# The start of a two-block transformer kernel: two product units formed from gained but unscaled x, with x loaded in chunks and the weight queue started at once

## The reference

```
def _rmsnorm(x, g, eps=EPS):
    xf = x.astype(jnp.float32)
    y = xf * lax.rsqrt(jnp.mean(xf * xf, axis=-1, keepdims=True) + eps)
    return (y * g.astype(jnp.float32)).astype(x.dtype)
...
        h = _rmsnorm(x, g_mix_pre[l])
        proj = h @ w_in[l]
...
    wl, al, gl = xs[..., o2:o3], xs[..., o3:o4], xs[..., o4:]
```

## Time and profile before

| what | us |
|---|---|
| median of 3 runs | 3977.71 (3976.71 to 3978.68) |
| the profiled execution | 3979.2 |
| its span | 3977.4 |
| TensorE busy | 3846.1 (97%) |
| VectorE, POOL, ScalarE busy | 1747.7, 1233.2, 599.5 |
| DMA moved | 668.80 MB, mean 168 GB/s |

### The profile page before, as it was taken

How to read it: one execution, slowest core, us unless ns; L and a number is a source line. 1 busy time by engine, 2 the same in 40 slices (tenths; PEclk the granted TensorE clock), 3 DMA queues, 4 the chain that set the end, 5 groups by cost and what they waited for, 6 DMA issues and landing times.

```text
span 3977.4 us, 65016 instructions
## 1 busy us (share of the span) xinstructions
PE 3846.1 (97%) x28196; PEld 3553.6 (89%) x28196; DVE 1747.7 (44%) x3073; ACT 599.5 (15%) x1314; POOL 1233.2 (31%) x779
## 2 busy tenths in 40 slices
PE   8999999999999998999999999989998899999997
PEld 7888888888878998999999998878797899999997
DVE  1344425550121623111125446552522688888544
ACT  0333311111111111000000000132402211111001
POOL 0000000003320865777760000000250577775000
PEclk9999999999999998999999999999999999999999
DMA  6566654457553443444445454428242344444542
GB/s 229 211 221 219 219 214 159 176 187 225 181 193 139 175 149 117 168 167 168 169 162 170 162 188 183 156 103 227 81 159 85 124 167 168 167 167 159 175 157 78
DMA packets 109117, 668.80 MB, mean 168 GB/s; under 512 B 23056, under 2 KB 27472, under 8 KB 78496
## 3 DMA queue, kind: packets, MB, share of 16 engines
q1 hardware_dynamic: 64208, 549.01, 38.2%
q0 software_dynamic: 21088, 69.73, 6.0%
q10 hardware_dynamic: 23536, 45.92, 3.2%
HBM read 611.34 MB, written 53.25 MB: 167 GB/s over the span
## 4 chain that ended last, share of the span: by engine, by line
PE 92%; DVE 3%; ACT 2%; issue 1%; POOL 1%; POOLq 1%; DVEq 1%; DMA 0%; ACTq 0%
PE product_bank L553 47%; PE product_bank L601 31%; PE product_bank L395 3%; PE mixer_bank L745 1%; PE mixer_bank L761 1%; ACT xT L862 0%; PE mixer_bank L1274 0%; PE mixer_bank L1288 0%; PE mixer_bank L1125 0%; POOL arena L525 0%; POOLq L524 0%; POOL arena L522 0%; POOLq L521 0%; PE product_bank L2237 0%; PE mixer_bank L2199 0%
## 5 line engine op out<-in xcount | busy, mean ns | idle before, releaser
L601 PE MATMUL product_bank<-hT,weight_ring 128*128 128x256 f32 x3712 | 825.0, 380 | 1.6 <-ACT out_stage L640 1.6
L601 PEld LDWEIGHTS product_bank<-hT,weight_ring 128*128 128x128 f32 x3712 | 700.6, 190 | 106.2 <-issue 12.0
L553 PE MATMUL product_bank<-hT,weight_ring 128*128 128x128 f32 x3648 | 453.6, 276 | 11.0 <-DVEq L1631 5.8
L553 PEld LDWEIGHTS product_bank<-hT,weight_ring 128*128 128x128 f32 x3648 | 432.2, 193 | 13.1 <-DVEq L1631 6.0
L553 PE MATMUL product_bank<-arena,weight_ring 128*128 128x128 f32 x3168 | 394.6, 275 | 0.0
L553 PEld LDWEIGHTS product_bank<-arena,weight_ring 128*128 128x128 f32 x3168 | 374.8, 192 | 0.6
L577 DVE TENSOR_TENSOR arena<-product_bank,arena 128x128 f32<-128x128 f32 x126 | 36.7, 291 | 721.1 <-PE product_bank L553 721.1
L520 POOL TENSOR_TENSOR arena<-weight_ring 128x1024 f32<-128x1024 f32 x88 | 211.0, 2398 | 449.7 <-PE product_bank L553 279.6
L2626 DVE SCALAR_TENSOR_TENSOR arena<-arena 128x256 f32<-128x256 f32 x176 | 321.8, 1867 | 14.6 <-ACT arena L2591 11.2
L523 POOL TENSOR_TENSOR weight_ring<-weight_ring 128x1024 f32<-128x1024 f32 x110 | 270.0, 2455 | 0.0
L553 PE MATMUL product_bank<-hT,arena 128*128 128x128 f32 x2016 | 247.4, 277 | 0.1
(11 more groups left out here) (494 smaller groups left out, 5303.5 us busy)
## 6 DMA issues: line engine op xcount, KB each, us to landing
weight_ring<-in_weights SPq DMA_DIRECT2D x213, 2048.0 KB, 8.0
weight_ring<-in_weights SPq DMA_DIRECT2D x128, 512.0 KB, 5.7
weight_ring<-in_weights SPq DMA_DIRECT2D x64, 384.0 KB, 5.7
units<-out_stage ACTq DMA_DIRECT2D x87, 256.0 KB, 7.8
rwkv_keep<-arena ACTq DMA_DIRECT2D x16, 1282.0 KB, 6.3
arena<-rwkv_keep POOLq DMA_DIRECT2D x8, 1280.0 KB, 7.2
arena<-units POOLq DMA_DIRECT2D x36, 256.0 KB, 3.4
arena<-units POOLq DMA_DIRECT2D x48, 128.0 KB, 6.0
```

Source lines behind the costliest of these rows:

```text
L553: mm = pe.matmul(bank[:, at * P:at * P + P], lhs[:, j, :], rhs[:, j, :], start=g == 0 and n in (0, 3) and j == 0, stop=g == n_groups - 1 a ...
L601: mm = pe.matmul(psg[b][:, half * T:half * T + T], lhs, rhs, start=k == 0, stop=k == 15)
```

## The change

1. SyncE no longer waits for x and the parameters. The load of slot 0 is split into four parts of 4 blocks each (4 KB per partition) with a semaphore each, `first_weights`; the other loads stay.
2. POOL loads the parameters first, then x in four chunks (4 KB per partition), each with its semaphore `x_loaded0` to `x_loaded3`, then the constants, as before in two parts.
3. VectorE (`first_norm_dve`) multiplies each chunk of x by the gains into `yT` as it lands.
4. TensorE (`first_units_pe`) forms lora unit 0 from `yT`, its first half chunk by chunk; then the sum of squares; then unit 1, from `yT` as well.
5. VectorE multiplies unit 0 by r as it puts it into `out_stage` (in place of ScalarE's copy), makes hT = yT * r with four instructions, puts unit 1 away. ScalarE (`store_first_units`) only stores.
6. TensorE waits for all four chunks of hT before rkv.

```diff
+        first_weights = [sem(f"first_weights{c}") for c in range(3)] + [w_ready[0]]
...
-                if isinstance(home, int):
+                if n == 0:
+                    for c in range(4):
+                        part = slice(SLOT // 4 * c, SLOT // 4 * c + SLOT // 4)
+                        sp.dma_start(ring[:, 0, part], weights[home, :, part]).then_inc(first_weights[c], 16)
+                elif isinstance(home, int):
...
-            pool.dma_start(xT[:, :, :], t_in["xT"]).then_inc(sem("x_loaded"), 16)
-            pool.dma_start(consts[:, 0:first], t_in["consts"][:, 0:first]).then_inc(sem("x_loaded"), 16)
             pool.dma_start(params[:, :], t_in["params"]).then_inc(sem("params_loaded"), 16)
+            for c in range(4):
+                pool.dma_start(xT[:, 4 * c:4 * c + 4, :], t_in["xT"][:, 4 * c:4 * c + 4, :]).then_inc(sem(f"x_loaded{c}"), 16)
+            pool.dma_start(consts[:, 0:first], t_in["consts"][:, 0:first]).then_inc(sem("norm_consts_loaded"), 16)
...
+        def first_units_pe(pe):
+            for u in range(2):
+                b, pos = PLAN["lora"].bank + u, PLAN["lora"].slot + u
+                if u:
+                    pe.wait_ge(sem("norm_consts_loaded"), 16)
+                    squares_pe(pe, "mix_pre", pm[0])
+                    pe.wait_ge(w_ready[pos % RING], READY[pos][0])
+                w = ring[:, pos % RING, :].rearrange("p (k n) -> p k n", n=256)
+                for half in range(2):
+                    for k in range(DB):
+                        if u == half == 0 and k % NB == 0:
+                            pe.wait_ge(sem("x_gained"), k // NB + 1)
+                            pe.wait_ge(first_weights[k // NB], 16)
+                        mm = pe.matmul(psg[b % 4][:, half * T:half * T + T], w[:, k, half * P:half * P + P], yT[:, k, :],
+                                       start=k == 0, stop=k == DB - 1)
+                mm.then_inc(w_used, 1)
+
+        def first_norm_dve(dve):
+            dve.wait_ge(sem("params_loaded"), 16)
+            for c, ck in enumerate(chunks_of):
+                dve.wait_ge(sem(f"x_loaded{c}"), 16)
+                for b in range(ck.start, ck.stop):
+                    last = dve.tensor_scalar(yT[:, b, :], xT[:, b, :], norm_param("g_mix_pre")[:, b:b + 1], None, ALU.mult)
+                last.then_inc(sem("x_gained"), 1)
+            r = reciprocal_dve(dve, "mix_pre")
+
+            def put_away(u):
+                b, o = (PLAN["lora"].bank + u) % 4, (PLAN["lora"].store + u) % RING
+                dve.wait_ge(w_used, PLAN["lora"].slot + u + 1)
+                dve.tensor_tensor(ostage[:, o, :].rearrange("p (h t) -> p h t", h=2),
+                                  psg[b][:, :].rearrange("p (h t) -> p h t", h=2), bc_b(r, 2), ALU.mult)\
+                    .then_inc(bank_free[b], 1)
+
+            put_away(0)
+            for ck in chunks_of:
+                dve.tensor_tensor(hT[:, ck, :], yT[:, ck, :], bc_b(r), ALU.mult).then_inc(sem("mix_in"), 1)
+            put_away(1)
+
+        def store_first_units(act):
+            for u in range(2):
+                row = PLAN["lora"].store + u
+                act.wait_ge(bank_free[PLAN["lora"].bank + u], 1)
+                act.dma_start(units[row, :, :], ostage[:, row % RING, :]).then_inc(stored[row % RING], 16)
...
         def _(sp):
-            sp.wait_ge(sem("x_loaded"), 32)
-            sp.wait_ge(sem("params_loaded"), 16)
             stream_weights(sp)
...
-            pe.wait_ge(sem("x_loaded"), 32)
-            squares_pe(pe, "mix_pre", pm[0])
-            products(pe, "lora", hT, ready="mix_in", count=NCK, chunks=NCK)
+            first_units_pe(pe)
+            pe.wait_ge(sem("mix_in"), NCK)
...
-            store_units(act, "lora")
+            store_first_units(act)
...
-            dve.wait_ge(sem("params_loaded"), 16)
-            dve.wait_ge(sem("x_loaded"), 32)
-            pre_norm_dve(dve, "mix_pre", "g_mix_pre", "mix_in")
+            first_norm_dve(dve)
```

More of the change, by code:

```diff
@@ L727, in squares_act @@
             for c, ck in enumerate(chunks_of):
-                act.wait_ge(sem(ready), count - NCK + 1 + c if ready != "x_loaded" else 32)
+                if tag == "mix_pre":
+                    act.wait_ge(sem(f"x_loaded{c}"), 16)
+                else:
+                    act.wait_ge(sem(ready), count - NCK + 1 + c)
                 act.activation(sq[:, ck, :], src[:, ck, :], ACT.Square).then_inc(sem("norm_squares"), 1)
```

## The result

| what | before | after |
|---|---|---|
| median of 20 runs each, us | 3977.64 | **3985.05** (3980.59 to 4008.6) |
| after / before, 95% interval | | 1.0024 (1.0015 to 1.0033) |
| the profiled execution | 3979.2 | 3983.77 |
| its span | 3977.4 | 3982.0 |
| first rkv matmul (the mark) | 56.06 | 59.28 |

The forecast was 3971.5 with the mark at 49.8 (48.2 if the clock held); the time lies outside the range, on the other side of before. Slower by a little over 0.2%. One of before's 20 runs took 6679 us and three of the 12 of e5_consts_later took over 8000: these are slow executions, and no ratio counts them.

The account below looks back on a forecast made before the run. TensorE, busy 97%, was taken as the bound. The first rkv matmul 7.9 us earlier, less 1.7 for a clock fall, gave -6.2: 3973.0 for the profiled execution, median 3971.5, range 3966.5 to 3976.0.

Parts of the forecast that it names:

- The place: First 56 us, up to the first rkv matmul: the only place where the change was to win time, 6.2 us.
- The sum behind chunk 3: TensorE from its start on x's last chunk to the first rkv matmul: 29.4 us with nothing missing.
- One row for one row: SyncE's and POOL's DMA queues alternate single rows whatever their size; x's last 5 rows cost 3.85 us.
- Everything that I cost at nothing: Root, reciprocal, putting unit 0 away, hT, other loads and issues: hidden under TensorE's work, 5.6 us of slack on `mix_in`.
- so its data flow from about 2.85, POOL's from about 3.3: Start of the load: SyncE's weight data flow from 2.85 us, POOL's from 3.3, so chunk 3 lands at 17.4.
- ahead of the flow: Each DMA load: some 3.0 us of overhead, 2 of it between issue and data flow, 1 behind.
- The clock: TensorE waits 2.4 to 3.2 us before chunk 3, then its clock falls, costing 1.7 us.
- rival 3: Start of the load: POOL's rows served last, behind all four slots, chunk 3 landing at 28.5; +5.9 us, chance 0.06.
- Its point of decision: Landing of x's chunk 3: the change makes the kernel slower if this comes later than about 24 us.
- rival 1: Start of the load: queues share by bytes, chunk 3 lands at 15.2, no clock loss; -10.1 us, chance 0.13.
- rival 2: Start of the load: whole DMAs take turns, chunk 3 lands at 19.1; about -4 us, chance 0.10.
- Rival 4: Behind 56 us: the clock falls after idle stretches, spending the won start; 0 to -3 us, chance 0.09.

Follow-up runs that it names:

- e5_consts_later: After, with parameters, x's chunks and slot 0's parts interleaved on SyncE's queue, POOL's constants held until x landed; median 3970.22 us, ratio to before 0.9978.
- e3: After, with slots 1 to 3 loaded in four parts each, rows of 4 KB instead of 16 KB; median 3972.03 us, ratio 0.9988.
- e2: After, with SyncE's waits for x, the norm's constants and the parameters put back ahead of its first load; median 3978.3 us, ratio 1.0009.
- e6: After, with TensorE multiplying an unused tile while it waits for each chunk of x; median 3982.8 us, ratio 1.0011.
- e7: e2 with 26 idle matmuls of TensorE ahead of chunk 0; median 3977.65 us, ratio 1.0001.
- e1: After, but SyncE waits for all four chunks of x between slot 0 and slot 1; median 3971.17 us, ratio 0.9988.
- e4: After, with x's chunks on SyncE's queue, each ahead of its part of slot 0, POOL keeping parameters and constants; median 3971.36 us, ratio 0.9982.
- after_b: After unaltered, traced once more; 3980.23 us.
- after_c: After unaltered, traced once more; 3984.68 us.
- after_a: After unaltered, traced once more; 3986.4 us.

## Why the prediction was wrong

**What held.** The place, in part: of the 4.6 us between the two traces 3.2 are there at the mark. The sum behind chunk 3, 29.4: e5 29.43, and after 31.78, with 2.36 of clock. One row for one row, which the sum rested on: 56 to 54, 24 to 23, and e3. Everything that I cost at nothing lay under other work: VectorE's root of the norm to the last hT ended at 53.2, 6.0 us ahead of the mark (5.6 foretold), TensorE waited for nothing at the squares, at unit 1 and at the mark, four gains took 1.14 together (foretold 1.35), the putting away 0.69 (0.7).

**The step that failed** is "so its data flow from about 2.85, POOL's from about 3.3". The 3.3 was POOL's issue at 1.27 and the 2 us "ahead of the flow", an estimate from whole loads of before, where no other queue was at work (POOL's packets there came 1.4 us after its issue). In after they came at 5.2, 3.9 us after it. The consequence is larger than those 1.9 us, since the sum changes rates when slot 0 is through. SyncE's queue had moved 0.93 MB, 14 rows of slot 0 per engine, by 5.2, not 3; slot 0 was read by 11 (and landed at 12.2, where 13.6 was foretold), and by then POOL had sent 14 rows of x per engine (228 of its 512), not 27. Eighteen rows were left, not 5. Eighteen at 0.77 is 13.9 in place of 3.85: read by 25, landed at 26.28.

How much of this is the start alone? The sum by its own rule, with 5.2 for 3.3: 15 rows of slot 0 alone, 17 pairs, slot 0 read by 10.6, 15 rows of x sent and 17 left; landed about 25, where it gave 17.4. So the start makes some 7.3 of the 8.9 us. The other 1.5 are smaller terms: slot 0 read by 11 for 10.6, one more row left, 1.3 us from the last row to the landing for 1. The row from which I took "one for one beside 4 KB" was good; the number of rows on either side of the change of price was not, and the range had no bound for POOL's start. One us of it at that place is 6 rows more of slot 0 that go alone, so 6 rows of x fewer in the cheap part: slot 0 is through 1 us earlier, the 6 rows cost 4.8 us, and chunk 3 lands 3.8 us later. That POOL's start moves with SyncE's queue is shown (e2 has 2.66); what makes it wait stays open.

**The clock.** Foretold was one wait of 2.4 to 3.2 and a fall at 1.7; there were two (4.16 and 3.05), and the clock was at 0.50 for 10.2 us, at the price of 2.36 on chunk 3's tail (e6: 2.3). The price follows from chunk 3's lateness, as its waits do.

**The rivals.** The time was near that of rival 3 (3983.6), by luck and not by its mechanism (it has all of +5.9 at the mark, which moved by 3.2): POOL's rows weren't served last but shared one for one from 5.2 on. Its point of decision, chunk 3 later than about 24, was right, and was passed (26.3). I gave it 0.06 for being unlikely as a rule of service, and did not ask what else would carry chunk 3 past 24. e3 rules out rival 1, the packets of 14.6 to 16.2 rival 2. Rival 4 stands, with both signs: late stretches moved single executions by up to some 6 us (e7: 5.9 ahead of before at 112, level at 3141). How much of after's median they make isn't shown.

**From the mark to the median.** Before's profiled execution lay 1.5 above its median, after's 1.3 below its own. So +4.6 between the profiled ones is +7.4 between the medians. Of that, 3.2 is the mark and 1.4 later stretches in this pair of traces. The five traced executions of after have 3983.77 as their middle, 6.1 above the median of before; the long runs, of which no trace exists, lift the median of 20 by a further 1. The rest cannot be assigned with one trace of before: that its trace is of the pattern without the falls near 2090 and 2540 doesn't say how often its runs are. It stays open.

## What to carry to other kernels

When two DMA queues run together, count rows and not bytes: a row of the stream that is waited for costs what the other queue's row costs, so hold back large rows until the small ones are in (e1), cut them (e3), or put all of it on one queue in the order of need (e5). A sum that changes its rate at an event has to be worked through with both bounds of the start of each queue, since a small delay there moves rows from the cheap part into the dear one: here each us of it came to 3.8 by the sum. The time saved by taking a wait out is that of what comes next: here the wait for x had kept the weights off the engines while x was on its way. And a start is worth what its mark says only within several us: later stretches moved the end of single executions by up to 6.

## What the runs showed of the hardware that I had not expected

- POOL's first packets came 1.4 us after its issue where its queue was the only one (2.66, before and e2), and 3.9 us after it where SyncE's queue had begun at 0.75 (5.2: after, e1). It isn't the loads of slots 1 to 3, which e1 issues only at 15.11, nor the number of POOL's own DMAs, of which e4 has three (first packet at 5.4). What does hold them back wasn't tried.
- POOL's queue shares with SyncE's one row for one whatever the size on either side (after, e3, e4 with POOL's the larger).
- An idle stretch of 4.16 us and one of 3.05 behind it left TensorE at 0.50 for 10.2 us; with 4.22 and 2.90 (after_b) and 2.98 and 2.70 (after_c) the mean over the same 10.2 us was 0.68 and 0.73, and the mark 0.7 to 0.8 earlier. Filled with idle work it stayed at 1.00 (e6).
- The same kernel follows one of two patterns of late clock falls: after_a, with falls near 2090 and 2540, goes from 2.5 behind before at 1880 to 5.8 at 2588, where after_b, without them, stays at 1.2.
